# Moving the sample group's steps half a block to a block later in the merged attention of a Trainium2 layer kernel

## What is computed

```
sc = einsum('bqhcd,bkhcd->bhcqk', q, k) * ATT_SCALE      # prompt: causal, in blocks of 128 queries
p  = softmax(sc)
w  = p[:, :, 0] - lam * p[:, :, 1]
o  = einsum('bhqk,bkhd->bqhd', w, v)
# samples: the same over concat(k_past[page_table], k_new), v likewise
```

## Time and profile before

| what | value |
|---|---|
| three runs | 2096.22, 2096.89, 2100.23 us; median 2096.89 us |
| the profiled execution | 2095.08 us, of it 2093.3 us the span of the profile |
| TensorE / VectorE / ScalarE busy over the span | 90% / 50% / 38% |
| the merged attention | 696.2 to 926.1 us of the span |
| starts of score in block 0 of heads 0 to 3 | 696.18, 745.65, 800.98, 855.97 us |

### The profile page before, as it was taken

One profiled execution on the slowest core, in us unless ns is written; L12 is line 12 of the kernel. 1 busy time (PEld: TensorE's weight loads), 2 busy tenths in 40 slices (PEclk: granted clock), 3 DMA queues, 4 the chain that ended last, 5 costly groups with the idle time before them and its releaser, 6 DMA issues.

```text
span 2093.3 us, 46480 instructions
## 1 busy us (share of the span) xinstructions
PE 1875.1 (90%) x19772; PEld 1781.1 (85%) x19772; DVE 1056.6 (50%) x1828; ACT 788.2 (38%) x1358; POOL 281.3 (13%) x288
## 2 busy tenths in 40 slices
PE   6999999599997488875499899999999999999996
PEld 5888888599996366664499899999999999999996
DVE  4355544235444466632326586654336766523655
ACT  4243323023320355531234555443335555422442
POOL 0011112069950000003000000000000000000000
PEclk9999999899999688886599999999999999999998
DMA  4234333620010877531124243323433422333343
GB/s 151 98 127 147 122 106 127 243 57 4 4 25 12 226 216 222 171 133 46 51 90 154 77 148 122 120 90 110 134 124 122 165 92 91 99 112 111 112 134 104
DMA packets 100620, 240.73 MB, mean 115 GB/s; under 512 B 14210, under 2 KB 18434, under 8 KB 100130
## 3 DMA queue, kind: packets, MB, share of 16 engines
q1 hardware_dynamic: 99554, 234.55, 35.0%
q10 hardware_dynamic: 864, 3.24, 0.4%
HBM read 189.54 MB, written 48.21 MB: 114 GB/s over the span
## 4 chain that ended last, share of the span: by engine, by line
PE 46%; DVE 2%; ACT 1%; issue 1%; DMA 0%; POOL 0%; SPq 0%; ACTq 0%; DVEq 0%
PE tl_acc L1970 44%; PE tl_ple L1970 1%; PE tl_wide L1945 0%; PE tl_wide L1936 0%; ACT tl_wh L2119 0%; DVE tl_tmp L2244 0%; DVE tl_gated L2307 0%; DVE tl_gated L2310 0%; DMA tl_raw<-dram_w_o 0%; ACT tl_sq_e L1982 0%; DVE tl_Y L2226 0%; DVE tl_Y L2217 0%; ACT tl_Hh L2088 0%; DVE tl_acc_e L2150 0%; DVE tl_wl L2290 0%
## 5 line engine op out<-in xcount | busy, mean ns | idle before, releaser
L1970 PE MATMUL tl_acc<-tl_Hh,tl_wh 128*128 128x264 f32 x1536 | 440.1, 287 | 7.3 <-DVE tl_Hl L2248 7.3
L1970 PE MATMUL tl_acc<-tl_Hh,tl_wl 128*128 128x264 f32 x1536 | 438.3, 285 | 0.0
L1970 PE MATMUL tl_acc<-tl_Hl,tl_wh 128*128 128x264 f32 x1536 | 438.2, 285 | 0.0
L2290 DVE TENSOR_TENSOR tl_wl<-tl_raw,tl_wh 128x1024 fp32r<-128x1024 f32 (+2 forms) x184 | 208.4, 1132 | 427.2 <-ACT tl_wh L2119 427.1
L2119 ACT ACTIVATE tl_wh<-tl_raw 128x1024 fp32r<-128x1024 f32 (+2 forms) x184 | 181.0, 984 | 503.0 <-PE tl_acc L1970 454.0
L1970 PEld LDWEIGHTS tl_acc<-tl_Hh,tl_wh 128*128 128x128 f32 x1536 | 290.3, 189 | 8.5 <-DVE tl_Hl L2248 8.3
L1970 PEld LDWEIGHTS tl_acc<-tl_Hh,tl_wl 128*128 128x128 f32 x1536 | 291.3, 190 | 0.0
L1970 PEld LDWEIGHTS tl_acc<-tl_Hl,tl_wh 128*128 128x128 f32 x1536 | 290.7, 189 | 0.0
L1970 PE MATMUL tl_acc<-tl_Gl,tl_wh 128*128 128x264 f32 x704 | 200.3, 285 | 0.0
L1970 PE MATMUL tl_acc<-tl_Gh,tl_wl 128*128 128x264 f32 x704 | 200.1, 284 | 0.0
L1970 PE MATMUL tl_acc<-tl_Gh,tl_wh 128*128 128x264 f32 x704 | 200.0, 284 | 0.0
(11 more groups left out here) (355 smaller groups left out, 4431.8 us busy)
## 6 DMA issues: line engine op xcount, KB each, us to landing
tl_raw<-dram_w_up SPq DMA_DIRECT2D x88, 512.0 KB, 3.6
as_kT<-dram_k_pool SPq DMA_DIRECT2D x64, 256.0 KB, 3.4
as_vp<-dram_v_pool SPq DMA_DIRECT2D x64, 256.0 KB, 3.0
tl_raw<-dram_w_down SPq DMA_DIRECT2D x32, 448.0 KB, 3.5
dram_projT<-fr_cur SPq DMA_DIRECT2D x26, 528.0 KB, 2.9
fr_raw<-dram_w_in SPq DMA_DIRECT2D x52, 256.0 KB, 3.6
tl_raw<-dram_w_pg SPq DMA_DIRECT2D x32, 320.0 KB, 3.2
ap_dup<-dram_projT SPq DMA_DIRECT2D x16, 512.0 KB, 8.5
```

The costliest lines, as they stand in the source:

```text
L1970: last = nc.tensor.matmul(out[:, n, 0:HP], w[:, u % 2, k, :], z, start=(begin and q == 0), stop=(end and q == 2))
L2290: tt(wl[:, u % 2, 0:kt], raw[:, u % 3, 0:kt], wh[:, u % 2, 0:kt].bitcast(F32), ALU.subtract).then_inc(S["residued"], 1)
```

## The change

The change reorders calls in three of the four loops of `attend`; no instruction is added or removed, no semaphore value and no buffer changes. VectorE's loop has one step more (U + 2 instead of U + 1) so that its last sample_fill has a place.

On TensorE, in terms of sample n with first block s = 4n: sample_scores(n, 0) goes from the end of step 4n+1 to behind score in step 4n+2; sample_scores(n, 1) from before values to behind values in step 4n+2; sample_scores(n, 2) from before turn to behind turn in step 4n+3; sample_turn(n) from before values to behind values in step 4n+4; sample_values(n) from before turn_v and turn to behind them in step 4n+5.

On VectorE: sample_peak(n) goes from the end of step 4n+3 (in the last block of a head it stood before low) to behind peak in step 4n+4; sample_combine(n) from before weight to behind it in step 4n+4; sample_fill(n) from the end of step 4n+4 to step 4n+5 between peak and weight.

On ScalarE: sample_move(n, 0) goes from before to behind the exponential in step 4n+2; sample_move(n, 1) from the same step to before the exponential in step 4n+3; sample_move(n, 2) from before to behind keep in step 4n+3; sample_exp(n) from the end of step 4n+3 (before split) to behind the exponential in step 4n+4. sample_leave stays.

```diff
 (TensorE, L956)
                 if s < U:
                     score(s)
-                if s % 4 == 3 and n < NB:
-                    sample_scores(n, 2)
-                if s % 4 == 1 and 1 <= n:
-                    sample_values(n - 1)
+                if s % 4 == 2 and n < NB:
+                    sample_scores(n, 0)
                 if s < U and s % NQ == 1:
                     turn_v(s)
                 if 2 <= s < U + 2:
                     turn(s - 2)
+                if s % 4 == 1 and 1 <= n:
+                    sample_values(n - 1)
+                if s % 4 == 3 and n < NB:
+                    sample_scores(n, 2)
+                if s >= 3:
+                    values(s - 3)
+                if s % 4 == 2 and n < NB:
+                    sample_scores(n, 1)
                 if s % 4 == 0 and 1 <= n:
                     sample_turn(n - 1)
-                if s % 4 == 2 and n < NB:
-                    sample_scores(n, 1)
-                if s >= 3:
-                    values(s - 3)
                 if s == 0:
                     turn_new()
-                if s % 4 == 1 and n < NB:
-                    sample_scores(n, 0)
 (VectorE, L1054)
-            for s in range(U + 1):
+            for s in range(U + 2):
                 n = s // 4
                 if s < U:
                     peak(s)
                 if s % 4 == 0 and 1 <= n:
+                    sample_peak(n - 1)
+                if s % 4 == 1 and 1 <= n:
+                    sample_fill(n - 1)
+                if 1 <= s < U + 1:
+                    weight(s - 1)
+                if s % 4 == 0 and 1 <= n:
                     sample_combine(n - 1)
-                if s >= 1:
-                    weight(s - 1)
...
-                if s % 4 == 0 and 1 <= n:
-                    sample_fill(n - 1)
-                if s % 4 == 3 and n < NB:
-                    sample_peak(n)
                 if s % NQ >= NQ - 4 and s // NQ + 1 < HEADS:
                     low(s // NQ + 1, s % NQ - (NQ - 4))
 (ScalarE, L1144)
+                if s % 4 == 3 and n < NB:
+                    sample_move(n, 1)
+                if s < U:
+                    exponential(s)
                 if s % 4 == 2 and n < NB:
                     sample_move(n, 0)
-                if s < U:
-                    exponential(s)
+                if s % 4 == 0 and 1 <= n:
+                    sample_exp(n - 1)
+                if 2 <= s < U + 2:
+                    keep(s - 2)
                 if s % 4 == 3 and n < NB:
                     sample_move(n, 2)
-                if 2 <= s < U + 2:
-                    keep(s - 2)
-                if s % 4 == 2 and n < NB:
-                    sample_move(n, 1)
                 if s % 4 == 1 and 1 <= n:
                     sample_leave(n - 1)
                 if s >= 3:
                     leave(s - 3)
-                if s % 4 == 3 and n < NB:
-                    sample_exp(n)
                 if s < U:
                     split(s)
```

## The result

The changed kernel takes 2118.57 us (median of 5 runs, 2116.29 to 2124.75), the kernel before 2097.09 in the same comparison. The ratio is 1.0096, 95% interval [1.0071, 1.0122]: slower, by about 20 us, where 8 were forecast, and 4.6 above the upper end of the range. In a later comparison 26 runs of the kernel before have a median of 2099.33 (2094.47 to 2109.77), so its profiled execution of 2095.08 was a short one; against that median the distance is 19 us.

What follows compares the result with a forecast made beforehand. TensorE and its gaps were taken to bound the attention. The terms, -4.1 + 3.3 + 2.4 + 6.2 + 1.2 + 2.7 - 1.9 - 4.3 + 2.4, sum to +7.9 us: 2104.8 against the median, predicted 2105, range 2097 to 2114.

Steps and rivals of the forecast that it cites:

- TensorE's clock: Three head boundaries and head 0: -4.3 us regained from the lower clock; block 4 of heads 2 and 3: +2.4 lost.
- End of a head and block 7: sample_peak leaves its place ahead of low, -1.35 us per head; late peak in block 7, +0.4 in heads 0 to 2.
- Block 0: Heads 1 to 3: late combine delays sample_turn; score of block 1 at +10.0 instead of +8.85, +3.3 us in all.
- Blocks 1 to 3: No cost: the 1.20 us wait stays, later value loads have slack, and the moves are ready in time.
- Block 4, heads 1 to 3: weight ahead of combine delays sample_turn by 1.6 us, values gives back 0.8: net +0.8 each, +2.4.
- Block 4, head 0: sample_exp stands behind the wait for the ap_dup DMA; score of block 5 at 729.4 instead of 723.20, +6.2 us.
- Blocks 5 and 6: Later sample_fill costs +0.3 us in each block 5, +1.2; in block 6 sample_scores(n, 1) waits 0.8 for the move.
- The end: End of the attention: last sample_turn starts 1.0 us later, but values goes ahead of it into the wait, -1.9.
- nearer to the row of 3.00: Head boundaries: reason for booking a clock gain of 1.0 us at each of three, between 0 and about 2.7.
- A: Block 0 of heads 1 to 3 and block 4: the clock holds; sum -5.6 us, 2091; chance 0.13.
- B: Blocks 5 to 7: VectorE sets a head's end, so late work is absorbed; +3 us, 2100; chance 0.2.
- C: Attention: new waits add up and the lower clock lasts longer after block 4; +15 us, 2112; chance 0.2.

Runs made afterwards that it cites:

- a_first: Changed kernel with sample 0's peak, exp, combine, turn and fill back at their old places; attention 236.0 us, ratio to the kernel before 1.0050.
- the two early loads: Load of ap_dup put ahead of sample 0's value pages, in the kernel before (attention 223.7 us, ratio 0.9979) and in the changed kernel (235.4, 1.0061).
- b_fill7: Kernel before with 30 added matmuls, results never read, in the last block of heads 0 to 2; attention 231.7 us, ratio 1.0000.
- b_fill_both: Kernel before with 14 unread matmuls added in block 7 of heads 0 to 2 and 12 in every block 4; attention 226.2 us, ratio 0.9974.

## Why the prediction was wrong, step by step

The direction was right and the sum of the waits too. The step that failed is the one headed "TensorE's clock": it booked 4.3 us as won back and 2.4 as lost, -1.9 in all, and TensorE's busy time for the same instructions rose by 6.4. The waits were forecast at 7.9 + 1.9 = 9.8 us, and its idle time rose by 10.8. Step by step, in lengths of blocks:

- *End of a head and block 7*: forecast -1.35, and +0.4 for the late peak, -0.95 for blocks 6 and 7 together. Measured +1.72 - 2.45 = -0.73 in each of heads 0 to 2. Right within 0.2 a head.
- *Block 0*: forecast +10.0 us with sample_turn at the lower level; 9.98 in heads 1 and 2. Right; in head 3 it is 9.53, with a wait of 1.75 and sample_turn at the upper level.
- *Blocks 1 to 3*: forecast nothing, measured +0.3, +1.3, +0.1 and +1.7 in heads 0 to 3, 3.4 in all. No wait is in this: TensorE's idle time in these blocks is the same within 0.15 us in all four heads. It is busy time, and the lower level lasts 2.9 and 4.8 us longer there in heads 1 and 3.
- *Block 4, heads 1 to 3*: forecast 0.8 each and 2.4 for the clock, 4.8 in all; measured 0.70, 1.84 and 2.25, sum 4.8. Right, the clock's term of 2.4 too: it was put in heads 2 and 3, and there it came.
- *Block 4, head 0*: forecast 6.2, measured 6.3; a_first and the two early loads show its cause.
- *Blocks 5 and 6*: +0.3 and a wait of 0.8 forecast; waits of 0.81 and 0.76 in head 1, block 5 +0.15 to +0.49 in heads 1 to 3, block 6 +1.7. Right.
- *The end*: forecast -1.9 beside +1.5 for the last peak and 1.7 from block 6; the last piece is 2.4 shorter, forecast 2.1. The size is right by luck: the wait ahead of sample_turn did not shrink (2.25 before, 2.19 after), and sample_turn itself took 2.12 instead of 3.81 because the clock was up, which the forecast did not count.
- *The clock*: 3.0 us were to come back at three head starts, and nothing did: block 0 came out at its length without them, and blocks 1 to 3 grew by 3.4. In head 0, 1.3 was to come back because I let the clock rise while score of block 5 ran. It stayed down for 23.4 us in all, through sample_values (3.64 us; 2.48 before), and block 5 took 1.5 longer instead of 1.0 shorter. These three, 3.0, 3.4 and 2.5, are 8.9 of the 9.3 us by which the attention was missed.

Why I had a price for the head starts at all: I read the clock in head 2 alone and called heads 1 and 2 alike. They are alike in their gaps, not in the clock: head 1 of the same trace has 10 us at the lower level where head 2 has 13, and 7 where it has 3. Gaps of equal length do not bring equal falls, so "nearer to the row of 3.00" was no price. Over all kernels the head starts with longer gaps have more of the lower level (10 to 13 us behind 5.0, about 7 to 13 behind 2.5, 7 to 10 behind 1.9, 3 where b_fill7 left no gap), but the spread at one length is as large as the 1.0 us a head that I had booked: block 1 takes 8.88 us in head 1 and 10.11 in head 2. Whether the new short waits in blocks 0, 5 and 6 keep the clock down longer is not shown by any run.

The Trainium skill (TensorE: Matmul & The Clock Gate, section Why this matters for your kernels) had been read as an argument for the change at the head starts. This case agrees with its advice to keep gaps short only where the gap at the head's start was filled whole: b_fill7 brought sample_turn from 3.69 to 2.12. Cutting the gap from 5.02 to 2.50 did not do it, with 13 us at the lower level in heads 1 and 2.

Of the rivals, A and B are out (the clock did not hold; late work was not absorbed). Two of their sums do not follow from their words. A's 13.5 has 8.4 us from block 4 in it, so at the head boundaries alone it would have been 5.1. C speaks of 2 to 3 us in each of three heads and adds 3 in all, beside the 2.4 of the forecast. C, waits that add up and a clock that stays low, had 15 us and came nearest to the 17.2; of the 15 us more at the lower level, though, some 10 are in head 0, which it did not name. The range missed because of the attention: 17.2 us on top of the median of 2099.33 are 2116.5, already above its end of 2114. Its signs came otherwise: waits for as_combs, as_wS and as_prob where they were named, and the score of block 5 in head 0 at 729.8, 729 being forecast. Only "nothing outside it moves" did not hold: 8 us moved there, of the size that comes and goes.

## What to carry to other kernels

A piece of a side chain that is done in the shadow of a long wait costs nothing there; before moving it behind the instruction that waits, add the whole chain to the wait (here 6.3 us, and 8.8 with the lower clock behind it). Shortening a gap pays less when a link of the same chain is next in line: here 0.8 of the 1.35 us won at one end was lost again at once. Where TensorE has gaps, count what its following work costs at the lower clock as well as the gap, and do not book a clock gain until rows of several such places show that such a gap goes without a fall; one place is not enough.

## What was not expected of the hardware

- Matmuls that compute nothing made the kernel faster: 14 and 12 of them per head in b_fill_both shorten the attention by 3.7 us, nearly all in one head, and the whole kernel by 5.7 (ratio 0.9974 [0.9959, 0.9989]). One takes 0.23 us at the upper clock (6.86 for 30).
- The lower level is not tied to the length of the gap before it: 10.1 and 13.3 us behind gaps of 5.03 and 5.02, 13.2 behind one of 2.50, and 3.2 in a place where the gap had been filled to 0.32. In the 13.2 us TensorE was busy for 12.24 and still did not get the upper level.
- The same kernel's runs spread over 15 us (2094.47 to 2109.77), the shortest at a mean granted clock of 0.939 and the longest at 0.934. The stretch from the attention to the next layer matmuls took 117.8 us in the profile of before, 81 of them at the lower level, and 122.8 in that of after, 92 of them at the lower level, with the same instructions; TensorE was busy for 58.3 and 63.9 of it. A profile of one execution carries some 5 us of this on a kernel of this kind; why it falls as it does in one execution and not in another stays open.
